# A hybrid SSD, attention and PEER block on one core: the gate's norm taken out of the turned operand, and three loads moved in SyncE's queue

## The reference, cut to what matters

```python
SEQ, D_MODEL = 512, 1024
PEER_HEADS, PEER_NKEYS, PEER_TOPK = 8, 128, 16            # 128*128 experts
def rms_norm(x, g):
    return x * rsqrt(mean(x * x, -1) + EPS) * g
def peer_ffn(xn, wq, sub_k1, sub_k2, expert_u, expert_v):
    ...                                                   # eidx, g: top-16 experts of each of 8 heads, per token
    act = gelu(einsum("td,thkd->thk", xt, expert_u[eidx]))
    return einsum("thk,thkd->td", act * g, expert_v[eidx])
h = x + concat(y_ssd, y_diff) @ w_out                     # SSD and attention mixer
h = h + peer_ffn(rms_norm(h, norm_ffn_g), ...)
e = rms_norm(p @ ple_proj, ple_norm_g)
gate = sigmoid(rms_norm(h, ple_gate_norm_g) @ ple_gate_w)
return h + gate * e
```

## Time and profile before

| | us |
|---|---|
| three timed runs | 1695.35, 1698.07, 1701.96 |
| median | 1698.07 |
| profiled execution, its own time | 1690.67 |
| its span, first to last instruction | 1688.9 |
| first pass, PE's 3072 matmuls at L1284 | 443.7 to 1086.5 |
| value stage, 2304 matmuls at L1330 | 1096.5 to 1621.3 |
| gate product | 1634.5 to 1684.2 |

### The profile page before, as it was taken

One profiled execution on the slowest core, in us unless ns is written; L12 is line 12 of the kernel. 1 busy time (PEld: TensorE's weight loads), 2 busy tenths in 40 slices (PEclk: granted clock), 3 DMA queues, 4 the chain that ended last, 5 costly groups with the idle time before them and its releaser, 6 DMA issues.

```text
span 1688.9 us, 26197 instructions
## 1 busy us (share of the span) xinstructions
PE 1605.9 (95%) x9085; PEld 1454.5 (86%) x9085; DVE 1170.9 (69%) x2513; ACT 620.7 (37%) x919; POOL 1077.1 (64%) x550
## 2 busy tenths in 40 slices
PE   7999878999799989999999999799999999999988
PEld 5799747877799988999999999788888888888878
DVE  6772574300879999958999996267667677577656
ACT  3133464211233323255555555323333333333331
POOL 5453303463368776867666665678888888889833
PEclk9999989999899999999999999999999999999989
DMA  5221103320368877858999998999999999999931
GB/s 197 75 85 66 53 36 116 150 75 25 115 212 306 282 251 244 274 194 317 341 341 352 333 350 296 323 348 346 370 350 367 355 354 361 360 354 357 374 144 44
DMA packets 172513, 417.74 MB, mean 247 GB/s; under 512 B 13088, under 2 KB 97696, under 8 KB 167328
## 3 DMA queue, kind: packets, MB, share of 16 engines
q1 hardware_dynamic: 133856, 257.52, 43.2%
q0 software_dynamic: 36864, 134.23, 22.2%
q10 hardware_dynamic: 1728, 25.17, 3.9%
HBM read 360.25 MB, written 56.62 MB: 247 GB/s over the span
## 4 chain that ended last, share of the span: by engine, by line
PE 55%; DVE 9%; issue 7%; DMA 1%; POOL 1%; SPq 1%; ACT 0%; DVEq 0%; POOLq 0%; ACTq 0%
PE s_psum L1330 29%; PE s_psum L1284 17%; PE s_psum L1310 5%; DVE h L1457 1%; PE s_psum L196 1%; DVE s_besti L1495 1%; DVE s_gtile L1489 1%; DVE s_besti L1486 1%; PE s_psum L197 1%; PE s_psum L198 1%; DVE s_gtile L1483 1%; DVE s_gtile L1492 1%; DMA s_gtile<-in_v_t,s_v_row 1%; POOL s_lo L1233 0%; DMA s_raw<-in_v_t 0%
## 5 line engine op out<-in xcount | busy, mean ns | idle before, releaser
L1233 POOL TENSOR_TENSOR s_lo<-s_raw,s_hi 128x1024 fp32r<-128x1024 f32 x224 | 538.1, 2403 | 225.5 <-ACT s_hi L1366 221.7
L1284 PE MATMUL s_psum<-hn_hi,s_hi 128*128 128x384 f32 x1024 | 351.1, 343 | 21.5 <-POOL s_lo L1233 21.4
L1366 ACT CAST s_hi<-s_raw 128x1024 fp32r<-128x1024 f32 x256 | 267.3, 1047 | 252.0 <-PE s_psum L1330 168.0
L1284 PE MATMUL s_psum<-hn_lo,s_hi 128*128 128x384 f32 x1024 | 345.6, 338 | 0.0
L1284 PE MATMUL s_psum<-hn_hi,s_lo 128*128 128x384 f32 x1024 | 345.5, 337 | 0.0
L1330 PE MATMUL s_psum<-s_hi,s_whi 128*128 128x512 f32 x768 | 299.9, 390 | 9.9 <-DVE s_wlo L1615 9.9
L1330 PE MATMUL s_psum<-s_lo,s_whi 128*128 128x512 f32 x768 | 299.7, 390 | 0.0
L1330 PE MATMUL s_psum<-s_hi,s_wlo 128*128 128x512 f32 x768 | 299.7, 390 | 0.0
L1267 POOL DMA_INDIRECT s_gtile<-in_v_t,s_v_row x128 | 212.6, 1661 | 25.0 <-issue 22.9
L1284 PEld LDWEIGHTS s_psum<-hn_hi,s_hi 128*128 128x128 f32 x1024 | 195.2, 191 | 24.7 <-POOL s_lo L1233 24.6
L1284 PEld LDWEIGHTS s_psum<-hn_lo,s_hi 128*128 128x128 f32 x1024 | 195.2, 191 | 0.0
(11 more groups left out here) (295 smaller groups left out, 2797.9 us busy)
## 6 DMA issues: line engine op xcount, KB each, us to landing
s_raw<-in_u_t SPq DMA_DIRECT2D x128, 512.0 KB, 4.9
s_raw<-in_v_t SPq DMA_DIRECT2D x128, 512.0 KB, 7.1
act_scratch<-s_acts SPq DMA_DIRECT2D x128, 192.0 KB, 4.5
gate_scratch<-s_gtile ACTq DMA_DIRECT2D x12, 2048.0 KB, 10.4
scores<-act_scratch SPq DMA_DIRECT2D x32, 768.0 KB, 7.0
scores<-gate_scratch SPq DMA_DIRECT2D x32, 768.0 KB, 10.2
m_w_raw<-in_w_in SPq DMA_DIRECT2D x11, 1024.0 KB, 4.8
m_w_raw<-in_w_q SPq DMA_DIRECT2D x8, 1024.0 KB, 4.8
```

Of the source, the lines that this page charges most:

```text
L1233: pool.tensor_tensor(lo[:, s, :], raw[:, s, :], hi[:, s, :].bitcast(F32), ALU.subtract).then_inc(lo_ready[s], 1)
L1284: last = pe.matmul(psU[:, s % 2, :], uu[:, s, d * P:(d + 1) * P], hh[:, d, P:T], start=(n == 0 and d == 0), stop=(n == 2 and d == DC - 1))
L1366: act.copy(hi[:, s, :], raw[:, s, :]).then_inc(hi_ready[s], 1)
```

## The change

Three edits, all in `experts_and_embedding`.

1. **The end.** `h` is turned as it is, without the norm (`xn` is gone). One square over a whole block in place of two halves goes into a junk tile, and the squares of blocks 1 to 3 stand behind the eight high-half copies. One root for the four blocks is taken afterwards; its reciprocal is the `scale` operand of the 16 sigmoids. DVE adds all blocks to `h` without a stop. A root of a single element loads ACT's table ahead.
2. **Bulk loads.** The second gate weight, `e` and `gain` wait in SP's queue until the last four sparse rows have landed.
3. **First value weights.** SP issues W0 between u125 and u126, and W1 behind v3. ACT makes the high half of W0 between the split of v1 and gelu 127.

```diff
-            with sp.Fori(1, turns) as it:
+            def load_scores(it, s):
+                sp.wait_ge(lo_ready[s], it)
+                sp.dma_start(raw[:, s, :], io["u_t"][it * UR + s]).then_inc(tile_loaded[s], 16)
+                store_acts(it * UR + (s - UR), s, it)
+
+            with sp.Fori(1, turns - 1) as it:
                 for s in range(UR):
-                    sp.wait_ge(lo_ready[s], it)
-                    sp.dma_start(raw[:, s, :], io["u_t"][it * UR + s]).then_inc(tile_loaded[s], 16)
-                    store_acts(it * UR + (s - UR), s, it)
-
+                    load_scores(it, s)
+            load_scores(turns - 1, 0)
+            load_scores(turns - 1, 1)
             for tile in range(2):
                 sp.wait_ge(gates_stored[tile], 16 * n_body)
             for s in range(UR):
+                sp.wait_ge(act_stored[s], 16)
+            load_weights(0, 0, 0)
+            load_scores(turns - 1, 2)
+            load_scores(turns - 1, 3)
+            load_values(0)
+            for s in range(UR):
                 sp.wait_ge(act_stored[s], 16 * 2)
-            load_weights(0, 0, 0)
             load_weights(1, 1, 0)
-            load_values(0)
...
-            for n in range(2):
-                g_weights.load(sp, n, io["w_gate"][n])
+            g_weights.load(sp, 0, io["w_gate"][0])
+            for k in range(UR):
+                sp.wait_ge(vrow_loaded[k], 16 * turns)
+            g_weights.load(sp, 1, io["w_gate"][1])
             sp.dma_start(e[:, :, :], e_dram.rearrange("t p d -> p t d")).then_inc(sem["e_loaded"], 16)
...
-            turn_blocks(pe, bank, "nT", sem["xn_ready"], 1, lambda t, c: xn[:, t, c * P:(c + 1) * P], ident)
+            turn_blocks(pe, bank, "nT", h_added, 2, lambda t, c: h[:, t, c * P:(c + 1) * P], ident)
...
-            with act.Fori(LOOP_C // UR, turns) as it:
+            with act.Fori(LOOP_C // UR, turns - 1) as it:
...
-            high_weights(0, 1, 0)
+            for s in range(UR):
+                split(turns - 1 + (s + 2) // UR, (s + 2) % UR)
+                if s == UR - 1:
+                    high_weights(0, 1, 0)
+                gelu(turns - 1, s)
...
-                    act.activation(xn[:, t, cs], h[:, t, cs], ACT.Square, accum_out=st[:, 0, t, half:half + 1]).then_inc(sem["sq_ready"], 1)
...
+            act.wait_ge(sem["one_set"], 1)
+            act.activation(hold[:, :], hold[:, :], ACT.Sqrt).then_inc(sem["one_set"], 1)
+
+            def square_of(t):
+                act.wait_ge(h_added, 2 * t + 2)
+                if t:
+                    act.wait_ge(sem["sq_ready"], t)
+                act.activation(junk[:, :], h[:, t, :], ACT.Square, accum_out=st[:, 0, t, 0:1]).then_inc(sem["sq_ready"], 1)
+
+            square_of(0)
             for c in range(DC):
                 src = bank.filled(act, "nT", c)
                 act.activation(nT_hi[:, c, :], src, ACT.Copy, scale=col(cols, C_GATE + c)).then_inc(sem["high_ready"], 1)
+            for t in range(1, TB):
+                square_of(t)
+            act.wait_ge(sem["ms_ready"], 1)
+            act.activation(st[:, 2, :, 0:1], st[:, 1, :, 0:1], ACT.Sqrt).then_inc(sem["root_ready"], 1)
+            act.wait_ge(sem["rstd_ready"], 1)
             for i in range(4 * TB):
                 src = bank.filled(act, "g", i)[:, 0:256]
-                act.activation(gate[:, i, :], src, ACT.Sigmoid).then_inc(sem["gate_ready"], 1)
+                act.activation(gate[:, i, :], src, ACT.Sigmoid, scale=st[:, 3, i % TB, 0:1]).then_inc(sem["gate_ready"], 1)
```

More of the change, by code:

```diff
@@ L1671, in step @@
                 me.settle()
[L1673 to L1679 removed]
             dve.wait_ge(h0_loaded, 16)
             dve.wait_ge(vrow_added[UR - 1], turns)
[L1683 to L1684 removed]
+            dve.memset(hold[:, :], 1.0).then_inc(sem["one_set"], 1)
+            for half in range(2):
+                hv = h[:, 0, half * 512:(half + 1) * 512]
+                dve.tensor_tensor(hv, hv, hn_dot[:, half * 512:(half + 1) * 512], ALU.add).then_inc(h_added, 1)
             dve.wait_ge(h_loaded, 16 * (TB - 1))
```

30 lines of the change are left out of this document (7 added, 23 removed).

## The result

| | before | after |
|---|---|---|
| median of 6 runs, us | 1695.35 | 1682.07 |
| lowest to highest | 1694.22 to 1701.96 | 1674.97 to 1687.68 |
| profiled execution, own time | 1690.67 | 1684.69 |
| its span | 1688.9 | 1682.7 |

The ratio of the medians is 0.9919, with a 95% interval of 0.9899 to 0.9940: the kernel is 0.8% faster, between 10 and 17 us. The forecast was 1687.8 us, in a range of 1680 to 1697.

A forecast was written before the change was run, and what follows sets the result against it. PE idle at the border of the passes and in the serial chain after the last value matmul was taken as the bound. 8.4 + 0 + 1.9 = 10.3 us off 1698.07 gave 1687.8, range 1680 to 1697 (own range 1685 to 1690.5).

The forecast's parts named there:

- The end, 8.4 us: After the last value matmul: serial norm chain leaves the path, gate product starts 4.8 us behind, not 13.2; gain 8.4.
- Rival D: At the end: clock falls before the transposes or late sigmoids hold banks; gain 5.8 there, 1690.4 us; chance 0.08.
- Bulk loads, 0: Held loads in SP's queue: cost and gain 0, bounds -0.5 to +0.5 us.
- The start, 7 us sooner: Border of the passes: PE's first value matmul starts near 1089.5 instead of 1096.5.
- rival C: SP's queue at the border: W0 ahead delays u126, PE stands 0.5 to 2 us; slower kernel, chance 0.05.
- The middle, 1.9 us: Value stage up to turn 2: 0.95 us of slack plus W2 landing 0.9 us sooner.
- The slack of 0.95 us: Before turn 2 of the value stage: low half ready 0.95 us early; the start's 7 us can't pass unless W2 comes sooner.
- with the same way from there to W2 (18.9 us): Value stage, from the end of `low_values` to W2's landing: 18.9 us as before, so W2 lands 0.9 us sooner.
- So everything hangs on W1: Early value turns: W1's landing seeds a loop of product, `low_values`, issue and W2's landing; each us counts one to one.
- the way of W2 was mostly queue: W2's load in the early value turns: 15.8 us of its way was queueing, argued for the start carrying through.
- Rival A: Value stage: start carries through, W2's way falls from 18.9 to 15 us, middle gains 7; 1682.7 us, chance 0.15.
- The sum, 10.3 us: Whole kernel: 8.4 + 0 + 1.9 us from end, bulk loads and first value weights, taken off a median of 1698.07.

The follow-up runs named there:

- squares_x9: Changed kernel with each of the three squares behind the copies made nine times; 1692.98 us in one execution.
- no_bulk: Changed kernel without the held bulk loads; 1680.30 us, ratio to before 0.9911.
- w1_early: Changed kernel with W1 loaded within the first pass, between v1 and v2, behind store 125; 1682.03 us, ratio to before 0.9905.
- h_late: Changed kernel with the loads of blocks 1 to 3 of `h` moved behind all value loads; 1679.50 us, ratio to before 0.9900.

## Why the prediction was right, and where it was wrong

**The end, 8.4 us: right in size and in cause.** 8.43 and 8.50 us were measured. Each piece of the sum is in the rows: the transposes at full clock with no idle time ahead (3.65 us for 32, had 3.86), the product at X + 4.55 for the 4.8 put down, the first gate tile at the pace of DVE's low halves (5.36 us as in the earlier trace rows). The six additions took 4.02 us and not 0.62 each, since they wait for PE's outputs, and still ended ahead of the transposes' need. The sigmoids were late and hidden: PE's first gate tile was done at 1633.22 and its sigmoid began at 1636.48, 3.2 us later for the 4 put down, with no wait of PE, and squares_x9 found the edge where the count of banks had put it. Rival D fell: the clock did not drop.

**Bulk loads, 0: right**, by no_bulk against after. The bounds of half a us held in the new end. In the old end X to end grew by 1 us in one execution, beside a clash of DVE with POOL that I had not looked for, and the timed runs don't show a loss.

**The start, 7 us sooner: 6.15.** The border stop was 2.21 us, within the 2 to 4 named. Of rival C there is a trace: u126 landed 2.5 us behind W0's gate part (G + 22.5 and G + 20.0), where 1.3 was put, and PE waited 1.29 us for it, where 0.5 to 2 was put. W1's product began at L = 1104.35, that is 9.75 us after the issue at 1094.60, for 9.3; counted from G it is 45.9 against the 44.8 that the forecast has (1098.3).

**The middle, 1.9 us: 2.75 in after and 4.3 in the mean, with one term mis-sized and the step on which it rests wrong.** That a part of the start is given back before turn 2 was right: in after 6.15 us came in and 2.75 were left. The slack of 0.95 us in the earlier trace rows fits. Only 2.5 us of stops came, not 5 to 8, since W2's product came 3.4 us sooner and not 0.9. The term that failed is "with the same way from there to W2 (18.9 us)": it took 15.5. With this the prediction's own sum is 0.95 + 3.4 = 4.35 us. The stop in this execution also cost 1.7 us of half clock behind it, which the sum didn't have; that leaves 2.65, for 2.75 measured. In the mean of the executions W2's product came 3.75 us sooner, which makes 4.7, for 4.3 measured.

**The causal step that failed is "So everything hangs on W1".** I read a loop of landing, product, `low_values` and issue out of the timeline, where each step does follow the one before, and took the landing as a fixed piece of it. w1_early moved the head of the chain by 9.3 us and its end by none. In this stretch, with a DMA share of 0.96 to 1.00, the way of W2 was no fixed latency but what had to go through before it; the 1.5 MB of `h` (4.5 us at 350 GB/s) and the gathers decide. The prediction had the hint, "the way of W2 was mostly queue", and used it as an argument for a rival only. Rival A had put this way at 15 us, and there it was right; but it had the whole 7 us of the start pass with it, and no execution of this order gave more than 5.4 against the mean of the old one. Against the expectation of h_late, its W2 came 6.9 us sooner and not 4.2. The windows show 2.4 MB less moved by then: 1.6 of `h`, and the rest agrees with the gathers, of which six had been issued by then and eight in after.

**The level, and what was luck.** The sum, 10.3 us, is 11.2 in the stages of the two profiled executions, 12.7 with the mean middle (8.4 + 4.3), and 13.3 in the medians, whose interval of 10 to 17 holds all of them. The sum was put on a median of three runs, 1698.07; with six it was 1695.35. Both errors went the same way: the level was 2.7 us too high and the gain 3.0 us too small, which is the 5.7 us between 1687.8 and 1682.07. The measured time lies in the stated range of 1680 to 1697, but outside the forecast's own range of 1685 to 1690.5 and 0.6 us from rival A's 1682.7. That closeness to A is chance: A's price for the middle, 7 us, was not measured. What was right in mechanism is the end, which is two thirds of the gain; the middle is right in sign and in its bound before turn 2, and wrong in what sets that bound.

## What to carry to other kernels

Before a chain of waits is read as cause and effect, see whether the DMA engines are full in it. If they are, a transfer that is issued sooner lands sooner only when fewer bytes go through before it: W1, issued 8.5 us sooner, was used 9.3 us sooner, but W2, issued 6.5 us sooner, came no sooner, since the same bytes and one MB of gathers more still went first. The lever is what may be taken out of the way (here 1.5 MB that nobody wanted for another 500 us). An early start of a stage is worth only the slack of its narrowest later place, so count back from the stage's end at the engine's own pace before valuing it; then remove what makes that place late. A per-row scale that commutes with a product belongs behind it, where the engine that applies it has time, and eight banks make seventeen us of such time here. A stage difference of a few us wants several executions on either side before it is laid to a cause.
